# A stick-breaking attention mixer on one core: mask and sums added to the logits in PSUM, exponentials taken from there

## The chip, the cores and the metric

The kernel runs on one core of one Trainium2 chip. The metric is the device time of one execution, in microseconds. Its engines are PE (TensorE, with PEld for its weight loads), DVE (VectorE), ACT (ScalarE), POOL (GpSimd) and SP (SyncE, which issues transfers here).

## The reference

Two networks of two layers each, over 256 tokens of width 1024, batch 1, float32. The change touches one mixer, in the first layer of the first network, with 16 heads of width 64:

```python
q, k, v = jnp.split(h @ w_qkv, 3, axis=-1)     # q, k normed per head
for blk in range(2):                           # 128 queries each
    z = einsum('bhqd,bhkd->bhqk', qb, kb) / 8  # keys 0 to the block's end
    causal = kpos[None, :] < qpos[:, None]
    log_stay = where(causal, log_sigmoid(-z), 0)
    log_after = cumsum(log_stay, reverse=True) - log_stay
    weights = where(causal, exp(log_sigmoid(z) + log_after), 0)
    outs.append(einsum('bhqk,bhkd->bhqd', weights, vb))
return o @ w_o
```

Around it stand gated feed-forward layers of inner width 2816; the second network has two other attentions and a mixture of 16384 experts.

## The kernel before, in words

Each engine has its own program, written out by hand; they meet only at semaphores, and each engine works its queue in order. Weights come in units of 128 x 1024 numbers through SP's queue into a ring of six (`raw`). ACT rounds each unit to a high part (L564), DVE subtracts it for the low part (L924), and a product is three matmuls per tile, high by high, low by high and high by low (`mm3`, L1518 to L1520). ACT may run four units ahead of PE. Meanwhile POOL moves expert weights through SBUF and back to HBM during the feed-forward layers (`relay`), but not during the mixer.

The mixer follows the q, k and v products. DVE squares and sums each head (`head_norm`, L1028 to L1037), PE turns q and k, and ACT copies them out with their gains (L609). Then comes `stick_breaking`, which each of PE, ACT, DVE and POOL has under this name. The scores are kept transposed: keys on the 128 partitions, and 384 columns per head, which are queries 0 to 255 for the first 128 keys and queries 128 to 255 for the last 128 keys. Heads go in pairs p = 0 to 7, so one call on ACT, DVE or POOL covers 2 x 384 = 768 numbers per partition.

For each pair: PE forms z (L1631, L1632) in three pairs of PSUM banks, in turn. ACT takes |z| (L659), exp(-|z|) (L660) and ln(1 + that) (L664), for two pairs at a time, so that the table of activation functions is changed twice for two pairs. DVE forms max(z, 0) + ln (L1061) and min(z, 0) - ln (L1063, `logw`). POOL multiplies the first by the causal mask (L485, `stay`). PE sums it over later keys with a triangular matrix and one of ones (L1646, L1647) in banks 0 and 1, and DVE takes the sums from `logw` (L1053). When all pairs are through, a second pass starts: ACT takes Exp (L669), POOL multiplies by the mask again (L490), PE mixes the values (L1658, L1659), ACT and DVE write the high and low parts of the output (L675, L1042). After the eighth the output product starts (L1518), whose first units were split long before.

A float32 matmul (scores, sums, mixes) appears in the trace as two records with a weight load each; a matmul of high and low parts as one. The second head of a pair has q and k on partitions 64 to 127, and its mixed output goes to partitions 64 to 127.

Of the kernel before, what the change touches and what calls it, by code (L numbers as in the profile page):

```python
# [31 lines left out]
P = 128  # L32
D = 1024
T = 256
# [20 lines left out]
STICK_GROUP = 2  # L55
# [18 lines left out]
A_STICKC = 27136  # L74
# [126 lines left out]
def program(nc, stream, x_in_dram, consts, stickc, poolc, scalec, ropec, lnc, subkeys, out):  # L201
    with ExitStack() as ctx:
# [24 lines left out]
        def sem(name):  # L227
            return ctx.enter_context(nc.semaphore(name))
# [40 lines left out]
        soft_done = sem("soft_done")  # L269
        z_used = sem("z_used")  # L270
        stay_ready = sem("stay_ready")
        c_done = sem("c_done")
        c_used = sem("c_used")
        w_exp = sem("w_exp")
        w_ready = sem("w_ready")
# [43 lines left out]
        def area(at, n):  # L319
            return arena[:, at:at + n]  # L320
# [22 lines left out]
        N_PAIRS = HEADS // 2  # L343
        near = pad[:, 0:HOT * 4 * NK].rearrange("p (s n) -> p s n", n=NK)
# [40 lines left out]
        def _(pool):  # L385
# [94 lines left out]
            def stick_breaking():  # L480
                m = area(A_STICKC, PAIR).unsqueeze(1).broadcast_to([P, 2, PAIR])
                soft = blk(A_SOFT, 4, PAIR)
                for p in range(N_PAIRS):
                    pool.wait_ge(soft_done, t.after(soft_done))
                    pool.tensor_tensor(stay[:, 2 * p:2 * p + 2, :], soft[:, 2 * (p % 2):2 * (p % 2) + 2, :], m,  # L485
                                       ALU.mult).then_inc(stay_ready, 1)
                for p in range(N_PAIRS):
                    pool.wait_ge(w_exp, t.after(w_exp))
                    w = logw[:, 2 * p:2 * p + 2, :]
                    pool.tensor_tensor(w, w, m, ALU.mult).then_inc(w_ready, 1)  # L490

            for i in range(DEPTH):
# [10 lines left out]
                if i == 0:  # L503
                    power(32, 64, 32)
                    power(32, 64, 32)
                    pool.wait_ge(stick_in, t.after(stick_in, 16))
                    stick_breaking()
# [39 lines left out]
        def _(act):  # L547
# [103 lines left out]
            def stick_breaking():  # L651

                ln = blk(A_LN, 8, PAIR)
                for first in range(0, N_PAIRS, STICK_GROUP):
                    group = range(first, first + STICK_GROUP)
                    for p in group:
                        act.wait_ge(z_done, t.after(z_done))
                        m = ln[:, 2 * (p % 4):2 * (p % 4) + 2, :]
                        step(act.activation(m, ps[:, 2 + 2 * (p % 3):4 + 2 * (p % 3), 0:PAIR], ACT.Abs))  # L659
                        ins = act.activation(m, m, ACT.Exp, scale=-1.0)  # L660
                    step(ins)
                    for p in group:
                        m = ln[:, 2 * (p % 4):2 * (p % 4) + 2, :]
                        act.activation(m, m, ACT.Ln, bias=cst[:, ONE:ONE + 1]).then_inc(ln_done, 1)  # L664
                for p in range(N_PAIRS + 1):
                    if p < N_PAIRS:
                        act.wait_ge(c_used, t.after(c_used))
                        w = logw[:, 2 * p:2 * p + 2, :]
                        act.activation(w, w, ACT.Exp).then_inc(w_exp, 1)  # L669
                    if p >= 1:  # L670
                        heads_high(p - 1, 4 + (p - 1) % 4)
# [237 lines left out]
        def _(dve):  # L909
# [134 lines left out]

            def stick_breaking():
                ln, soft = blk(A_LN, 8, PAIR), blk(A_SOFT, 4, PAIR)

                def log_weights(p):

                    dve.wait_ge(z_used, t.after(z_used))  # L1050
                    dve.wait_ge(c_done, t.after(c_done))
                    w = logw[:, 2 * p:2 * p + 2, :]
                    dve.tensor_tensor(w, w, ps[:, 0:2, 0:PAIR], ALU.subtract).then_inc(c_used, 1)  # L1053

                for p in range(N_PAIRS):
                    s, r = slice(2 * (p % 2), 2 * (p % 2) + 2), slice(2 * (p % 4), 2 * (p % 4) + 2)
                    z = ps[:, 2 + 2 * (p % 3):4 + 2 * (p % 3), 0:PAIR]
                    dve.wait_ge(ln_done, t.after(ln_done))
                    if p >= 2:
                        dve.wait_ge(stay_ready, t.after(stay_ready))  # L1060
                    dve.scalar_tensor_tensor(soft[:, s, :], z, 0.0, ln[:, r, :], ALU.max,  # L1061
                                             ALU.add).then_inc(soft_done, 1)
                    dve.scalar_tensor_tensor(logw[:, 2 * p:2 * p + 2, :], z, 0.0, ln[:, r, :], ALU.min,  # L1063
                                             ALU.subtract).then_inc(z_used, 1)
                    if p >= 1:
                        log_weights(p - 1)
                t.skip(stay_ready, 2)
                log_weights(N_PAIRS - 1)
                for p in range(N_PAIRS):
                    heads_low(p, 4 + p % 4)  # L1070
# [74 lines left out]
            for i in range(DEPTH):  # L1145
# [360 lines left out]
        def _(pe):  # L1506
# [113 lines left out]
            def stick_breaking():  # L1620
                mask_tri = area(A_STICKC + PAIR, P)
                ones = area(A_STICKC + PAIR + P, P)
                pe.wait_ge(turned_kept, t.after(turned_kept, 8))
                pe.wait_ge(stick_in, 16)

                def scores(p):
                    if p >= 3:
                        pe.wait_ge(z_used, t.after(z_used))
                    for h in range(2):
                        z, r = ps[:, 2 + 2 * (p % 3) + h, :], slice(64 * h, 64 * h + 64)  # L1630
                        pe.matmul(z[:, 0:T], kT[r, p, 0:P], qT[r, p, 0:T], start=True, stop=True)  # L1631
                        ins = pe.matmul(z[:, T:PAIR], kT[r, p, P:T], qT[r, p, P:T], start=True, stop=True)  # L1632
                    ins.then_inc(z_done, 1)

                for p in range(3):
                    scores(p)
                for p in range(N_PAIRS):
                    if p + 3 < N_PAIRS:
                        scores(p + 3)

                    pe.wait_ge(stay_ready, t.after(stay_ready))
                    if p >= 1:
                        pe.wait_ge(c_used, t.after(c_used))
                    for h in range(2):
                        c, s = ps[:, h, :], stay[:, 2 * p + h, :]
                        pe.matmul(c[:, 0:PAIR], mask_tri, s, start=True, stop=False)  # L1646
                        ins = pe.matmul(c[:, P:T], ones, s[:, T:PAIR], start=False, stop=True)  # L1647
                    ins.then_inc(c_done, 1)
                t.skip(c_used)
                pe.wait_ge(z_used, t.after(z_used, 3))  # L1650
                for p in range(N_PAIRS):
                    pe.wait_ge(w_ready, t.after(w_ready))
# [459 lines left out]
```

## Time and profile before

| | us |
|---|---|
| median of 3 timed runs | 2883.92 (2879.01 to 2887.53) |
| profiled execution | 2879.02 |
| its span | 2877.1 |
| PE busy in the span | 2573.6 (89%) |
| DVE busy | 2004.7 (70%) |
| ACT busy | 1261.3 (44%) |
| POOL busy | 1170.8 (41%) |
| mean granted clock of PE | 0.963 |

The span runs from the first to the last instruction of the profiled execution; the profiled execution's own time holds what lies around it. The busy time of PE comes from matmul records that overlap, with ends that are modelled, so it says where PE is at work and not how near it is to its peak. A granted clock of 1.00 is 2.4 GHz, 0.50 is 1.2 GHz.

### The profile page before, as it was taken

The numbers are of one execution on the slowest core, as the hardware profiler recorded it, in microseconds if no ns is written. First come the engines' busy times: TensorE is split into PE (matmuls) and PEld (weight loads), VectorE is DVE, ScalarE is ACT, GpSimd is POOL, SyncE is SP. The second block draws the span as 40 slices with busy tenths as digits, with TensorE's granted clock in tenths as the row PEclk, the third lists the DMA queues.
The fourth block names the chain that finished last, engine by engine and source line by source line (L and its number), as shares of the span: only waits on it lengthen the run. The fifth ranks groups of instructions, "written<-read, shape, count | busy, mean of one in ns | idle before, by whom it ended". The sixth has DMA issues, their size and how long they took to land.

```text
span 2877.1 us, 41657 instructions
## 1 busy us (share of the span) xinstructions
PE 2573.6 (89%) x14180; PEld 2073.2 (72%) x14180; DVE 2004.7 (70%) x3942; ACT 1261.3 (44%) x2087; POOL 1170.8 (41%) x1498
## 2 busy tenths in 40 slices
PE   8999799989989987899999889999986778887776
PEld 8987589879979976699999878888774333333322
DVE  6775466756767665498899657676676767777675
ACT  5445644444444445455555445554553222222221
POOL 3531444424415431048788733332102444444442
PEclk9999899999999998799999999999898999999999
DMA  9985189989959997255555599999746999999997
GB/s 356 366 299 170 43 321 365 333 326 368 352 198 351 378 336 266 91 162 184 183 183 183 165 361 387 392 393 339 270 138 262 422 420 409 421 407 419 418 418 307
DMA packets 217960, 874.90 MB, mean 304 GB/s; under 512 B 38320, under 2 KB 38448, under 8 KB 184176
## 3 DMA queue, kind: packets, MB, share of 16 engines
q0 software_dynamic: 118640, 512.52, 46.0%
q1 hardware_dynamic: 99200, 360.96, 35.3%
q8 instruction: 54, 0.88, 0.1%
q14 instruction: 66, 0.54, 0.1%
HBM read 788.27 MB, written 152.17 MB: 327 GB/s over the span
## 4 chain that ended last, share of the span: by engine, by line
PE 56%; DMA 14%; POOL 12%; DVE 9%; ACT 4%; issue 4%; SPq 0%; POOLq 0%; DVEq 0%; ACTq 0%
PE ps L1518 16%; PE ps L1519 16%; PE ps L1520 16%; DMA arena<-both_rows,arena 12%; POOL gate_cells L447 11%; PE ps L1892 5%; DVE arena L1428 2%; DVE w_lo L924 1%; DMA raw<-in_stream 1%; PE ps L1673 1%; ACT arena L728 1%; ACT w_hi L564 1%; DVE pad L1364 0%; POOL small L391 0%; DVE act_lo L952 0%
## 5 line engine op out<-in xcount | busy, mean ns | idle before, releaser
L924 DVE TENSOR_TENSOR w_lo<-raw,w_hi 128x1024 fp32r<-128x1024 f32 x681 | 829.8, 1223 | 441.3 <-ACT w_hi L564 436.7
L564 ACT ACTIVATE w_hi<-raw 128x1024 fp32r<-128x1024 f32 x681 | 719.1, 1057 | 617.1 <-DMA raw<-in_stream 420.4
L1518 PE MATMUL ps<-act_hi,w_hi 128*128 128x256 f32 x2728 | 781.3, 286 | 7.7 <-DVE act_lo L958 3.6
L1519 PE MATMUL ps<-act_lo,w_hi 128*128 128x256 f32 x2728 | 773.7, 284 | 0.0
L1520 PE MATMUL ps<-act_hi,w_lo 128*128 128x256 f32 x2728 | 773.7, 284 | 0.0
L1892 PE MATMUL ps<-arena 128*128 128x512 f32 x1024 | 480.9, 616 | 149.0 <-ACT arena L728 148.2
L1518 PEld LDWEIGHTS ps<-act_hi,w_hi 128*128 128x128 f32 x2728 | 525.1, 192 | 18.8 <-issue 12.6
L1519 PEld LDWEIGHTS ps<-act_lo,w_hi 128*128 128x128 f32 x2728 | 525.3, 193 | 5.8 <-issue 2.6
L1520 PEld LDWEIGHTS ps<-act_hi,w_lo 128*128 128x128 f32 x2728 | 525.0, 192 | 0.0
L1892 PEld LDWEIGHTS ps<-arena 128*128 128x128 f32 x1024 | 189.2, 194 | 428.9 <-ACT arena L728 234.7
L419 POOL DMA_DIRECT2D both_rows<-arena x512 | 279.2, 552 | 411.1 <-DVE arena L990 401.2
L477 POOL DMA_INDIRECT arena<-both_rows,arena x256 | 288.4, 1126 | 385.6 <-PE ps L1892 351.0
L1428 DVE SCALAR_TENSOR_TENSOR arena<-arena 128x1024 f32<-128x1024 f32 x256 | 313.1, 1225 | 167.6 <-DMA arena<-both_rows,arena 165.9
L1518 PE MATMUL ps<-w_hi,act_hi 128*128 128x512 f32 (+1 forms) x990 | 388.3, 392 | 30.2 <-DVE act_lo L1487 16.3
L1519 PE MATMUL ps<-w_lo,act_hi 128*128 128x512 f32 (+1 forms) x990 | 385.7, 390 | 0.0
L1520 PE MATMUL ps<-w_hi,act_lo 128*128 128x512 f32 (+1 forms) x990 | 385.1, 389 | 0.0
L447 POOL DMA_INDIRECT gate_cells<-hot x256 | 317.4, 1240 | 121.4 <-issue 80.8
L1518 PEld LDWEIGHTS ps<-w_hi,act_hi 128*128 128x128 f32 x990 | 190.2, 192 | 73.5 <-issue 17.3
L721 ACT ACTIVATE hot<-hot 128x2 f32<-128x2 f32 (+1 forms) x130 | 26.4, 203 | 468.0 <-DVE arena L1428 467.3
L1520 PEld LDWEIGHTS ps<-w_hi,act_lo 128*128 128x128 f32 x990 | 189.6, 192 | 38.4
L1519 PEld LDWEIGHTS ps<-w_lo,act_hi 128*128 128x128 f32 x990 | 190.0, 192 | 37.3
L465 POOL DMA_DIRECT2D both_rows<-in_stream x128 | 68.1, 532 | 295.6 <-DMA both_rows<-in_stream 295.6
(237 smaller groups left out, 2793.5 us busy)
## 6 DMA issues: line engine op xcount, KB each, us to landing
raw<-in_stream SPq DMA_DIRECT2D x684, 512.0 KB, 5.8
arena<-in_stream POOLq DMA_DIRECT2D x128, 512.0 KB, 8.9
both_rows<-arena POOLq DMA_DIRECT2D x512, 128.0 KB, 5.9
both_rows<-in_stream POOLq DMA_DIRECT2D x128, 512.0 KB, 6.7
gate_cells<-hot POOLq DMA_DIRECT2D x32, 512.0 KB, 13.0
hot<-gate_cells POOLq DMA_DIRECT2D x128, 128.0 KB, 6.7
pad<-in_ln POOLq DMA_DIRECT2D x4, 1024.0 KB, 7.4
gate_cells<-hot POOLq DMA_INDIRECT x256
```

Source lines behind the costliest of these rows:

```text
L419: pool.dma_start(rows.rearrange("(c r) k -> r c k", r=32), arena[32 * a:32 * a + 32, A_RELAY_OUT + UNIT * s:A_RELAY_OUT + UNIT * s + UNIT] ...
L447: pool.indirect_dma_start(gate_cells[:, :], bass.IndirectOffsetOnAxis(ap=cell[:, q:q + 1], axis=0), weights[:, q:q + 1], None).then_inc(sc ...
L465: pool.dma_start(both_rows[P * n:P * n + P, D:2 * D], stream[UP_1 + n]).then_inc(up_copied[n % 2], 16)
L477: pool.indirect_dma_start(row[:, p % ROW_RING, :], None, both_rows[:, :], at).then_inc(row_in[p % ROW_RING], 16)
L564: act.activation(w_hi[:, u % SPLIT, :], raw[:, u % RAW, :], ACT.Copy).then_inc(hi_done, 1)
L728: act.activation(diags[:, p % DIAG_RING, :], ident, ACT.Copy, scale=weights[:, p:p + 1]).then_inc(diag_ready, 1)
L924: dve.tensor_tensor(w_lo[:, u % RAW, :], raw[:, u % RAW, :], w_hi[:, u % SPLIT, :].bitcast(F32), ALU.subtract).then_inc(lo_done, 1)
L1428: dve.scalar_tensor_tensor(row[:, p % ROW_RING, 0:D], row[:, p % ROW_RING, 0:D], 1.0, x_rows[:, b, :], ALU.mult, ALU.mult, accum_out=dots[ ...
L1518: pe.matmul(dst, lhs[0], rhs[0], start=first, stop=False, **kw)
L1519: pe.matmul(dst, lhs[0], rhs[1], start=False, stop=False, **kw)
L1520: return pe.matmul(dst, lhs[1], rhs[0], start=False, stop=last, **kw)
L1892: ins = pe.matmul(ps[:, 2 * (n % 2) + half, :], diags[:, p % DIAG_RING, :], row[:, p % ROW_RING, D + 512 * half:D + 512 * half + 512], sta ...
```

## The change

The logits stay in PSUM until their last use. There are four pairs of banks; pair p has pair p mod 4 of them, 384 columns of each bank for the logits and the last 128 for the output. PE adds to the logits a third matmul per head, a unit matrix times a matrix that is -2^99 where the key is not before the query. DVE writes the size of the masked logit to SBUF by clearing its sign bit (two shifts as integers); ACT takes Exp and Ln of it in place; DVE forms max(z, 0) + ln straight into `stay`, which is 0 where the mask is. PE then adds minus the sums onto the logits themselves, with a triangular matrix that includes the key's own term, so that z minus its own softplus is formed there too. ACT takes Exp from PSUM, which is the weights, and 0 where the mask is. PE mixes the values into the free columns of the same banks, in three matmuls per head, not two. Abs, the second expression on DVE, the subtraction of the sums and both multiplications on POOL are gone.

ACT goes over four pairs with each function: Exp four times, Ln four times, Exp four times with the copies between. PE forms the logits of pairs 0 to 3, then alternates sums and mixes; the logits of pairs 4 to 7 wait for the outputs of pairs 0 to 3 to have left the banks. Four small operations on DVE (`stick_terms`), before the head norms, build the matrices.

The diff is cut: removed lines that stand in the listing above are left out.

```diff
-A_STICKC = 27136
+A_STICKC, A_TERMS = 27136, 27776
...
+        stick_ring = blk(A_LN, 8, PAIR)
+        neg_tri, neg_ones = area(A_TERMS, P), area(A_TERMS + P, P)
+        neg_mask, unit_mat = in_place("neg_mask", [P, P], base + 4 * (A_TERMS + 2 * P)), in_place("unit_mat", [P, P], base + 4 * (A_TERMS + 3 * P))
+        def logit(p):
+            r = 2 * (p % 4)
+            return ps[:, r:r + 2, 0:PAIR]
+        def mixed(p):
+            r = 2 * (p % 4)
+            return ps[:, r:r + 2, PAIR:PAIR + P]
+        def sizes(p):
+            return stick_ring[:, 2 * (p % 4):2 * (p % 4) + 2, :]
...
-            def stick_breaking():
...
-                    pool.tensor_tensor(stay[:, 2 * p:2 * p + 2, :], soft[:, 2 * (p % 2):2 * (p % 2) + 2, :], m,
...
-                    pool.tensor_tensor(w, w, m, ALU.mult).then_inc(w_ready, 1)
...
-                    stick_breaking()
...
+                def weights_of(p):
+                    act.wait_ge(c_done, p + 1)
+                    act.activation(logw[:, 2 * p:2 * p + 2, :], logit(p), ACT.Exp).then_inc(w_exp, 1)
+                def output_high(p):
+                    act.wait_ge(o_done, t.after(o_done))
+                    act.activation(act_hi[:, p, :].rearrange("p (b q) -> p b q", b=TB), mixed(p),
+                                   ACT.Copy).then_inc(o_hi, 1)
+                for first in (0, 4):
+                    group = range(first, first + 4)
                     for p in group:
...
+                        act.wait_ge(size_done, p + 1)
+                        ins = act.activation(sizes(p), sizes(p), ACT.Exp, scale=-1.0)
                     step(ins)
                     for p in group:
...
+                        act.activation(sizes(p), sizes(p), ACT.Ln, bias=cst[:, ONE:ONE + 1]).then_inc(ln_done, 1)
+                    for p in group:
+                        weights_of(p)
+                        if p > first:
+                            output_high(p - 1)
+                    output_high(first + 3)
...
+            def stick_terms():
+                dve.wait_ge(stick_in, 16)
+                ahead = area(A_STICKC, P)
+                dve.tensor_scalar(neg_tri, ahead, -1.0, None, ALU.add)
+                dve.tensor_scalar(neg_mask[:, :], ahead, -1.0, 2.0 ** 99, ALU.add, ALU.mult)
+                dve.tensor_scalar(neg_ones, area(A_STICKC + PAIR + P, P), -1.0, None, ALU.mult)
+                dve.tensor_copy(unit_mat[:, :], ident).then_inc(terms_ready, 1)
             def stick_breaking():
...
+                def size(p):
+                    dve.wait_ge(z_done, p + 1)
+                    dve.tensor_scalar(sizes(p).bitcast(U32), logit(p).bitcast(U32), 1, 1, ALU.logical_shift_left,
+                                      ALU.logical_shift_right).then_inc(size_done, 1)
+                def stays(p):
+                    dve.wait_ge(ln_done, p + 1)
+                    dve.scalar_tensor_tensor(stay[:, 2 * p:2 * p + 2, :], logit(p), 0.0, sizes(p), ALU.max,
+                                             ALU.add).then_inc(stay_ready, 1)
+                def output_low(p):
+                    dve.wait_ge(o_hi, t.after(o_hi))
+                    dve.tensor_tensor(act_lo[:, p, :].rearrange("p (b q) -> p b q", b=TB), mixed(p),
+                                      act_hi[:, p, :].bitcast(F32).rearrange("p (b q) -> p b q", b=TB),
+                                      ALU.subtract).then_inc(act_ready, 1)
+                for p in range(4):
+                    size(p)
+                for p in range(4):
+                    stays(p)
+                for p in range(3):
+                    output_low(p)
+                size(4)
+                output_low(3)
+                for p in range(5, 8):
+                    size(p)
+                for p in range(4, 8):
+                    stays(p)
+                for p in range(4, 8):
+                    output_low(p)
...
+                    stick_terms()
...
             def stick_breaking():
...
                 pe.wait_ge(turned_kept, t.after(turned_kept, 8))
...
+                pe.wait_ge(terms_ready, 1)
+                def logits(p):
                     if p >= 4:
                         pe.wait_ge(act_ready, t.after(act_ready))
                     for h in range(2):
...
+                        z, r = logit(p)[:, h, :], slice(64 * h, 64 * h + 64)
+                        same = z.rearrange("p (c q) -> p c q", q=P)[:, 0:3:2, :]
+                        pe.matmul(z[:, 0:T], kT[r, p, 0:P], qT[r, p, 0:T], start=True, stop=False, skip_group_check=True)
+                        pe.matmul(z[:, T:PAIR], kT[r, p, P:T], qT[r, p, P:T], start=False, stop=False,
+                                  skip_group_check=True)
+                        ins = pe.matmul(same, unit_mat[:, :], neg_mask[:, :].unsqueeze(1).broadcast_to([P, 2, P]),
+                                        start=False, stop=False, skip_group_check=True)
+                    ins.then_inc(z_done, 1)
+                def sums(p):
+                    pe.wait_ge(stay_ready, p + 1)
+                    for h in range(2):
+                        z, s = logit(p)[:, h, :], stay[:, 2 * p + h, :]
+                        pe.matmul(z, neg_tri, s, start=False, stop=False, skip_group_check=True)
+                        ins = pe.matmul(z[:, P:T], neg_ones, s[:, T:PAIR], start=False, stop=True, skip_group_check=True)
+                    ins.then_inc(c_done, 1)
+                def mix(p):
+                    pe.wait_ge(w_exp, p + 1)
+                    for h in range(2):
+                        e, v = logw[:, 2 * p + h, :], slice(HD * (2 * p + h), HD * (2 * p + h) + HD)
+                        o = mixed(p)[64 * h:64 * h + 64]
+                        pe.matmul(o[:, 0, :], v_tok[:, 0, v], e[:, 0:P], start=True, stop=True, skip_group_check=True)
+                        pe.matmul(o[:, 1, :], v_tok[:, 0, v], e[:, P:T], start=True, stop=False, skip_group_check=True)
+                        ins = pe.matmul(o[:, 1, :], v_tok[:, 1, v], e[:, T:PAIR], start=False, stop=True,
+                                        skip_group_check=True)
                     ins.then_inc(o_done, 1)
+                for p in range(4):
+                    logits(p)
+                sums(0)
+                sums(1)
+                mix(0)
+                sums(2)
+                mix(1)
+                sums(3)
+                mix(2)
+                logits(4)
+                mix(3)
+                for p in (5, 6, 7):
+                    logits(p)
+                sums(4)
+                sums(5)
+                mix(4)
+                sums(6)
+                mix(5)
+                sums(7)
+                mix(6)
+                mix(7)
```

## Rows read from the trace of the kernel before

**Rows 1.** The page's chain that ended last, shares of the span by engine.

```profile
PE 56%; DMA 14%; POOL 12%; DVE 9%; ACT 4%; issue 4%; SPq 0%; POOLq 0%; DVEq 0%; ACTq 0%
```

**Rows 2.** Chain of waits, end of the mixer: start us, us, what.

```profile
334.13 1.81 POOL arena L490
338.50 0.79 PE ps L1518
```

**Rows 3.** Groups by line and shape, 283.5 to 338.5: line, engine, form | busy us, mean ns | idle.

```profile
L485 POOL TENSOR_TENSOR arena<-arena 128x768 f32<-128x768 f32 x8 | 14.5, 1815 | 35.4 <-DVE arena L1061 35.4
L1061 DVE SCALAR_TENSOR_TENSOR arena<-ps,arena 128x768 f32<-128x768 f32 x8 | 7.6, 953 | 15.2 <-ACT arena L664 15.2
L664 ACT ACTIVATE arena<-arena,cst 128x768 f32<-128x768 f32 x8 | 7.0, 926 | 0.0
L660 ACT ACTIVATE arena<-arena 128x768 f32<-128x768 f32 x8 | 6.7, 843 | 0.2
L659 ACT ACTIVATE arena<-ps 128x768 f32<-128x768 f32 x8 | 6.4, 798 | 1.0 <-PE ps L1632 1.0
L660 ACT ACT_TABLE_LOAD x4 | 5.1, 1283 | 0.1
L1042 DVE TENSOR_TENSOR act_lo<-ps,act_hi 128x256 fp32r<-128x256 f32 x8 | 3.4, 425 | 11.9 <-ACT act_hi L675 11.9
L675 ACT ACTIVATE act_hi<-ps 128x256 fp32r<-128x256 f32 x8 | 3.1, 383 | 13.0 <-PE ps L1659 13.0
```

**Rows 4.** Busy time by stretch: us, then PE, PEld, DVE, ACT, POOL; PE's granted clock; DMA.

```profile
284.30:293.20 8.90, 2.88 (x20) 2.59 (x16) 1.83 (x3) 8.54 (x10) 0.72 (x1) 0.51 0.00 1
293.20:298.05 4.85, 4.80 (x15) 3.21 (x16) 1.72 (x2) 4.78 (x6) 2.86 (x2) 0.50 0.00 2
298.05:322.00 23.95, 17.68 (x92) 11.98 (x90) 17.07 (x19) 19.40 (x21) 13.48 (x8) 1.00 0.00 0
322.00:332.20 10.20, 4.84 (x45) 2.87 (x46) 3.08 (x6) 5.47 (x10) 8.20 (x6) 1.00 0.01 2
332.20:338.50 6.30, 3.81 (x23) 1.84 (x19) 1.27 (x3) 1.88 (x4) 3.52 (x2) 0.50 0.00 0
338.50:342.40 3.90, 3.90 (x9) 3.13 (x10) 0.00 (x0) 0.00 (x0) 0.00 (x0) 0.50 0.00 0
```

**Rows 5.** PE's instructions in order of time, same records merged: start us, us, form, count.

```profile
283.56 0.71 PE L1631 MATMUL ps<-arena 64*128 64x256 f32 x4 [2.66 <-ACT arena L609]
298.35 0.71 PE L1631 MATMUL ps<-arena 64*128 64x256 f32 x4
298.88 0.39 PE L1632 MATMUL ps<-arena 64*128 64x128 f32 x4
299.62 0.88 PE L1646 MATMUL ps<-arena 128*128 128x384 f32 x2 [0.35 <-DVE arena L1053]
301.53 0.71 PE L1631 MATMUL ps<-arena 64*128 64x256 f32 x4
322.00 0.66 PE L1658 MATMUL ps<-arena 128*64 128x256 f32 x4
322.48 0.40 PE L1659 MATMUL ps<-arena 128*64 128x128 f32 x4
```

**Rows 6.** ACT in order of time, at the next feed-forward layer's first Silu.

```profile
371.60 1.28 ACT L639 ACT_TABLE_LOAD   x1
376.60 0.38 ACT L639 ACTIVATE arena<-ps 128x256 f32<-128x256 f32 x1 [3.72 <-PE ps L1520]
```

**Rows 7.** PE in order of time, inside a product with 256 columns.

```profile
149.75 0.28 PE L1519 MATMUL ps<-act_lo,w_hi 128*128 128x256 f32 x1
149.87 0.28 PE L1520 MATMUL ps<-act_hi,w_lo 128*128 128x256 f32 x1
```

**Rows 8.** POOL and DVE in order of time, ahead of the mixer.

```profile
205.35 0.60 POOL L499 DMA_DIRECT2D arena<-in_stick  x1 [0.15 <-issue]
235.40 2.29 DVE L1028 TENSOR_TENSOR arena<-arena 128x2048 f32<-128x2048 f32 x1 [0.60 <-ACT arena L619]
```

More of the change, by code:

```diff
@@ L268, in program @@
         ln_done = sem("ln_done")
-        soft_done = sem("soft_done")
-        z_used = sem("z_used")
+        terms_ready = sem("terms_ready")
+        size_done = sem("size_done")
         stay_ready = sem("stay_ready")
         c_done = sem("c_done")
-        c_used = sem("c_used")
         w_exp = sem("w_exp")
-        w_ready = sem("w_ready")
         o_done = sem("o_done")
@@ L478, in gather @@
                                                 at).then_inc(row_in[p % ROW_RING], 16)
-            def stick_breaking():
[L481 to L484, printed above, removed]
-                    pool.tensor_tensor(stay[:, 2 * p:2 * p + 2, :], soft[:, 2 * (p % 2):2 * (p % 2) + 2, :], m,
[L486 to L489, printed above, removed]
-                    pool.tensor_tensor(w, w, m, ALU.mult).then_inc(w_ready, 1)
             for i in range(DEPTH):
@@ L651, in stick_breaking @@
             def stick_breaking():
-                ln = blk(A_LN, 8, PAIR)
-                for first in range(0, N_PAIRS, STICK_GROUP):
-                    group = range(first, first + STICK_GROUP)
+                def weights_of(p):
[7 more added lines that the diff above has]
+                    group = range(first, first + 4)
                     for p in group:
[L657 to L660, printed above, removed]
+                        act.wait_ge(size_done, p + 1)
+                        ins = act.activation(sizes(p), sizes(p), ACT.Exp, scale=-1.0)
                     step(ins)
                     for p in group:
[L663 to L671, printed above, removed]
+                        act.activation(sizes(p), sizes(p), ACT.Ln, bias=cst[:, ONE:ONE + 1]).then_inc(ln_done, 1)
[4 more added lines that the diff above has]
+                    output_high(first + 3)
             def heads_high(k, bank):
@@ L1043, in heads_low @@
                                   ALU.subtract).then_inc(act_ready, 1)
-            def stick_breaking():
[L1046 to L1070, printed above, removed]
@@ L1620, in stick_breaking @@
             def stick_breaking():
-                mask_tri = area(A_STICKC + PAIR, P)
-                ones = area(A_STICKC + PAIR + P, P)
                 pe.wait_ge(turned_kept, t.after(turned_kept, 8))
[L1624 to L1652, printed above, removed]
+                pe.wait_ge(terms_ready, 1)
+                def logits(p):
                     if p >= 4:
@@ L1655, in stick_breaking @@
                     for h in range(2):
-                        o, e = ps[64 * h:64 * h + 64, 4 + p % 4, :], logw[:, 2 * p + h, :]
-                        v = slice(HD * (2 * p + h), HD * (2 * p + h) + HD)
-                        pe.matmul(o[:, 0:T], v_tok[:, 0, v], e[:, 0:T], start=True, stop=False)
-                        ins = pe.matmul(o[:, P:T], v_tok[:, 1, v], e[:, T:PAIR], start=False, stop=True)
-                    ins.then_inc(o_done, 1)
+                        z, r = logit(p)[:, h, :], slice(64 * h, 64 * h + 64)
```

2 lines of the change are left out of this document (removed).

## The prediction

> **What bounds the kernel now.** The page comes first. Its chain of waits [rows 1] gives PE 56% of the span; the rest is transfers and POOL in the later layers. The change touches one stage of one layer, so everything is decided between its first matmul (L1631, at 283.56 us in the instructions in order of time [rows 5]) and the first matmul of the product after it (L1518, at 338.50 in the chain of waits of that stretch [rows 2]): 54.94 us, 1.9% of the span. Grouped by line [rows 3], that stretch holds 8 calls of each form, one per head pair. ACT works 8 x (0.80 + 0.84 + 0.93) plus eight table loads of 1.28 (four at L660, as many at L664; one more at L669 later) between the first score and the last Ln, and is idle for 1.0 us: it bounds the first 31 us. Then POOL bounds: the second multiplication by the mask (L490, 1.81 each) is on the chain to 335.94 [rows 2]. PE is not the bound anywhere here. The granted clock [rows 4] fell to half (1.2 GHz) at 284.3, just after a pause of 2.66 us [rows 5]; it stayed there through 8.9 us in which PE worked 2.9, and rose at 298.05, when PE had worked without a stop since 293.2 (4.85 us). It fell again at 332.2, after 10.2 us with PE at work for 4.8, and rose at 342.4, 3.9 us into the product. DMA moves nothing in the stretch, and nothing behind it waits for an absolute time: what the stage gains, the kernel gains.
>
> **The change, part by part.**
>
> *POOL.* All 16 multiplications leave (8 x 1.82 [rows 3], and 8 of L490's 1.81 [rows 2]). The first eight lay beside ACT's work; the second eight were the bound of the last 16 us. Nothing else is moved past POOL's queue.
>
> *ACT.* Abs leaves (8 x 0.80). Exp of the size, Ln, Exp of the weights and the copies stay: 8 x (0.84 + 0.93 + 0.80 + 0.38) = 23.6. For the Exp that now reads PSUM I take L659's 0.80, which reads the same shape from there. Table loads: nine now (4 + 4 + 1), five after: Exp, Ln, Exp, Ln, Exp. A load does not wait for what its activation waits for: at L639 it ran at 371.60 and the activation came at 376.60, once PE was done [rows 6]. So the first Exp load hides behind the first logits, and those ahead of the weights behind PE's sums. Two loads, both before Ln, stay on the path. The Trainium skill (ScalarE: Activation LUTs, What ACT_TABLE_LOAD costs) gives a switch 2.66 us, as a load of 1283 ns and a drain of about 1380. The rows give 1283 ns and no drain: the activations and loads of groups of two pairs fill ACT's time. With the drain the change would save about 1.4 us more for each of seven loads that leave the path, some 10 us; this is a rival below. The same page (Table sets) says that one set holds both exp and ln; this program reloads at each turn, so the rule earns nothing here.
>
> *DVE.* L1063 and L1053 leave, the sign-clearing of 768 numbers from PSUM comes, L1061 stays. The trace has no integer shift of that size; the nearest rows are L1061 (768 from PSUM, 0.95) and L1042 (256, 0.43), so it lies between 0.8 and twice 0.95; I take 0.95. It matters only once per half. DVE has 8 x (0.95 + 0.95 + 0.43) = 18.6 us, and is no bound. The four small operations of `stick_terms` (128 columns each) cost at most 4 x 0.43, L1042's price for 256. They wait for a table that was issued at 205.4, 30 us earlier, and stand in the 0.60 us in which DVE idles ahead of L1028 at 235.40 [rows 8]. What overflows, up to 1.1 us, delays a square and the lows of the k weights, which run ahead of PE. I count nothing; without that cover it is 1.1 us.
>
> *PE.* A new load. Sums: from L1646 at 299.62 to L1631 at 301.53 a pair takes 1.91 [rows 5]; unchanged. Mixes: 0.88 a pair, from 322.00 to 322.88, the last record's tail of about 0.15 in it; the same columns in 12 passes rather than 8, so 0.75 to 1.2; I take 0.85. Logits: now the two heads of a pair lie in different halves of the array, and both run at once: four records of each kind fit into 298.35 to 299.27 [rows 5], about 0.75 without the tail. The change puts a full-height matmul (the mask, 256 columns) behind each head. One such matmul with its weights takes 0.12 (149.75 to 149.87 [rows 7]), so two take 0.24. If the heads no longer overlap, 384 columns at the sums' rate (1.91 us for 2 x 512 columns, so 0.70 for 384) make 2 x 0.70 + 0.24 = 1.64 a pair; if they still do, 1.0. Upwards, each of four changes of tile shape may cost the 0.1 that stands at the head of a run, so 2.04. I take 1.64. The Trainium skill (PSUM — Partial Sum Buffer, Engine vs sequencer instructions) says that matmuls start and complete in program order. By that the mask stands between the heads and 1.64 holds. The records speak half against it: the source issues head 0 wholly before head 1, yet the four L1631 come before the four L1632, so something ahead of the array had put them in turn. By this the price would be 1.0.
>
> *The clock.* Low stretches: the fall at 284.3 comes from what PE did before the change's first matmul, and stays. Each long PE pause makes another. I take each to last 4.4 us of steady work (between 3.9 and 4.85 [rows 4]), which costs 2.2.
>
> *The path*, since PE, ACT and DVE now take turns:
> a. Four pairs of logits: 4 x 1.64 + 2.2 = 8.8, to 292.3. ACT and DVE follow pair by pair beneath.
> b. Size of pair 3 (0.95), its Exp (0.84), the Ln load (1.28), the first Ln (0.93), the first `stays` (0.95), hand-overs 0.3: 5.25, to 297.6. PE stands still throughout.
> c. Four sums, four mixes, logits 4: 4 x 1.91 + 4 x 0.85 + 1.64 + 2.2 = 14.9, to 312.5. Each Exp of weights (0.80) fits under the next sums.
> d. Logits 5, 6, 7: 4.9, to 317.4. Each has its bank: the low halves of pairs 1 to 3 end before.
> e. As b: 5.25, to 322.7.
> f. Four sums, four mixes: 11.0 + 2.2 = 13.2, to 335.9.
> g. Last copy 0.38, last difference 0.43, hand-overs 0.3: to 337.0.
> The stage takes 53.4 instead of 54.9: -1.5. The product then starts with PE warm: its first 3.9 us at half clock [rows 4] gave up 1.95. Together -3.5 us. The profiled execution (2879.02, span 2877.1 and 1.9 around it) would become 2875.5. It equals the fastest of the three timed runs and lies 4.9 below their median; on the median the forecast is 2883.9 - 3.5 = 2880.4. So most of what ACT and POOL gave up goes to PE, with twice a chain of 5.25 us in which nothing overlaps.
>
> **The rivals.**
> 1. *The heads still run side by side.* 8 x 0.64 = 5.1 less on the path: 8.6 gained, 2875.3; with a shorter low stretch up to 11. For it: the order of the records [rows 5]. Against: a full-height matmul needs both halves in between.
> 2. *PE becomes the bound at half clock.* Place: logits 0 to 3. Half-height matmuls did not lift the clock in 284.3 to 293.2, though PE was at work for 2.9 us. If one head's half doesn't either, part a takes 0.7 + 2 x (6.56 - 0.7) = 12.4 instead of 8.8, and the gain is gone: 2883.9. From there each 0.1 a pair adds about 1.2; with 2.04 a pair the loss is about 5: 2889. It decides from 1.64 a pair and a low stretch over all four. Against it: PE has no pause in those 8 us.
> 3. *The change doesn't do what it says*: loads of tables not merged or not hidden, or the shift twice as long: two Exp loads and two sizes more on the path, 2 x 1.3 + 2 x 0.95 = 4.5 slower than forecast, 2884.9.
> 4. *A drain at each load leaves the path too*: 2871. The skill's figure speaks for it, the full ACT rows against.
>
> **How the numbers follow.** Forecast 0.50 (2877.5 to 2883.5), rival 1 0.20, rival 2 0.20, rival 3 0.07, rival 4 0.03. No change can be told from one under 0.3%, or 8.65 us, here. Half of rival 1 and all of rival 4 lie beyond it: faster 0.13. Slower takes a corner of rival 2 and the scatter of medians: 0.07. The rest, 0.80, is the same. The range is 2873 to 2889.
>
> **What would show it.** In the profile after: nothing of POOL in the stage; five table loads; PE idle for about 5 us twice, between the fourth logits and the first sums of each half; 1.6 us between the z of two pairs at full clock (1.0 for rival 1, over 1.9 for the high bound); the first sums at half clock; the product's first matmuls at full clock and about 53 us behind the first logits. A half clock up to 293 is rival 2. The prediction is wrong if the stage shrinks by over 7 us or grows, or if the time moves with the stage unchanged.

## The result, and the profile after

The changed kernel took 2894.91 us (median of 10 runs, 2884.32 to 2899.33) and the kernel before 2885.41 (10 runs, 2879.01 to 2890.69): a ratio of 1.0032, 95% interval 1.0016 to 1.0048. It is slower by 9.5 us, which is 0.3% and clear of the scatter, and outside the forecast's range of 2873 to 2889. The profiled execution took 2897.5, with a span of 2895.7.

Busy time by stretch in the profile after, with the columns of [rows 4]: six parts of the stage as the prediction cut it (a, b, c, d, e, f with g), the whole stage, and the product behind it up to the additions to x.

```profile
286.20:302.40 16.20, 16.20 (x40) 11.19 (x40) 2.87 (x3) 3.76 (x4) 0.00 (x0) 0.52 0.00 0
302.40:307.50 5.10, 0.01 (x1) 0.00 (x0) 1.90 (x3) 4.04 (x5) 0.00 (x0) 0.50 0.01 2
307.50:323.20 15.70, 15.63 (x90) 11.21 (x90) 4.82 (x8) 7.17 (x10) 0.00 (x0) 0.90 0.00 1
323.20:332.10 8.90, 8.90 (x31) 6.33 (x30) 2.35 (x4) 2.80 (x4) 0.00 (x0) 0.75 0.00 0
332.10:337.30 5.20, 0.07 (x1) 0.00 (x0) 1.94 (x3) 4.07 (x5) 0.00 (x0) 0.50 0.00 0
337.30:352.00 14.70, 13.77 (x80) 9.84 (x80) 4.27 (x7) 7.53 (x11) 0.00 (x0) 0.86 0.00 0
286.18:352.03 65.85, 54.60 (x240) 38.59 (x240) 18.15 (x24) 29.39 (x37) 0.00 (x0) 0.71 0.00 0
352.03:373.80 21.77, 21.77 (x96) 17.94 (x96) 8.58 (x8) 7.42 (x7) 0.00 (x0) 1.00 0.51 162
```

The stage took 65.85 us where it had taken 54.94: 10.9 more. The product took 21.77; in the trace of before it is this:

```profile
338.50:362.09 23.59, 23.59 (x96) 19.28 (x96) 8.58 (x8) 7.42 (x7) 0.00 (x0) 0.92 0.47 151
```

So 1.82 came back, at full clock from its first matmul. The sum, +9.1, is near the 9.5 between the medians. (The two profiled executions differ by 18.5; 2.6 of it lies ahead of the stage and 6.9 behind the product, in code that the change leaves alone.) POOL has nothing left in the stage. ACT, which bounded its first 31 us, is busy for 29.4 of 65.9 and PE for 54.6 (it was 34.8).

PE's instructions in order of time in the profile after, with the columns of [rows 5]: the first heads, then logits 4 and the first mix behind it.

```profile
286.18 0.70 PE L1651 MATMUL ps<-arena 64*128 64x256 f32 x2 [2.66 <-ACT arena L608]
286.71 0.57 PE L1652 MATMUL ps<-arena 64*128 64x128 f32 x2
287.22 0.58 PE L1654 MATMUL ps<-neg_mask,unit_mat 128*128 128x256 f32 x1
287.73 1.22 PE L1651 MATMUL ps<-arena 64*128 64x256 f32 x2
288.74 0.63 PE L1652 MATMUL ps<-arena 64*128 64x128 f32 x2
289.31 0.58 PE L1654 MATMUL ps<-neg_mask,unit_mat 128*128 128x256 f32 x1
289.82 1.22 PE L1651 MATMUL ps<-arena 64*128 64x256 f32 x2
...
320.99 0.70 PE L1651 MATMUL ps<-arena 64*128 64x256 f32 x2
321.53 0.38 PE L1652 MATMUL ps<-arena 64*128 64x128 f32 x2
321.84 0.38 PE L1654 MATMUL ps<-neg_mask,unit_mat 128*128 128x256 f32 x1
322.15 0.43 PE L1671 MATMUL ps<-arena 128*64 128x128 f32 x2
```

The reader is to see two things. In [rows 5] four L1631 stand in one record and four L1632 in the next: both heads of a pair ran at once. Here two stand together, then two, then a mask: one head wholly before the other. And a head takes 2.09 us at half clock (287.73 to 289.82) and 1.16 at full (320.99 to 322.15), so a pair takes 4.18 or 2.32.

### The profile page after: what moved, and what is told of

It is laid out like the page before. It is cut to its first block, busy times and chain, and to the rows that moved or that the text cites. A ratio compares the mean times of both kernels' runs of the same rounds, so it can differ in the third digit from the quotient of the medians.

```text
span 2895.7 us, 41694 instructions
## 1 busy us (share of the span) xinstructions
PE 2597.0 (90%) x14228; PEld 2092.9 (72%) x14228; DVE 1996.0 (69%) x3938; ACT 1250.7 (43%) x2075; POOL 1141.8 (39%) x1482
## 4 chain that ended last, share of the span: by engine, by line
PE 57%; DMA 14%; POOL 12%; DVE 9%; issue 4%; ACT 4%; SPq 0%; POOLq 0%; DVEq 0%; ACTq 0%
PE ps L1537 16%; PE ps L1538 16%; PE ps L1539 16%; DMA arena<-both_rows,arena 12%; POOL gate_cells L460 11%; PE ps L1929 4%; DVE arena L1447 2%; DMA raw<-in_stream 1%; PE ps L1710 1%; DVE w_lo L926 1%; ACT w_hi L563 1%; ACT arena L730 1%; PE ps L1651 1%; PE ps L1662 1%; ACT arena L598 0%
## 5 line engine op out<-in xcount | busy, mean ns | idle before, releaser
L1537 PEld LDWEIGHTS ps<-act_hi,w_hi 128*128 128x128 f32 x2728 | 527.1, 193 | 17.8 <-issue 12.5
L1537 PEld LDWEIGHTS ps<-w_hi,act_hi 128*128 128x128 f32 x990 | 189.5, 191 | 75.5 <-issue 21.3
L404 POOL TENSOR_TENSOR small<-small,cst 128x1 f32<-128x1 f32 (+2 forms) x27 | 26.9, 998 | 475.7 <-DVE small L936 394.2
```

Source lines behind the costliest of these rows:

```text
L1537: pe.matmul(dst, lhs[0], rhs[0], start=first, stop=False, **kw)
```

## The experiments

"The stage" is always the stretch from its first logits (or scores) matmul to the first matmul of the product, in the profiled execution; it was 54.94 before and 65.85 after. It is compared between all kernels, and it is one execution each, so a difference of 2 us between two stages can be chance (see "When the clock rises" below). Times are compared only with the runs of the kernel before on the same chip: on the chip of the first seven kernels these took about 2985 us, on those of the last four about 2884.

The theory: the mask between the two heads of a pair puts them one after the other, and PE, at work with one half-height head at a time, doesn't bring its clock up. The rivals: the two mask matmuls are dear in themselves; the clock was low from before and only stays so; four pairs per table make a hand-over that is too long.

**Masks behind both heads.** The same matmuls in another order:

```diff
     for h in range(2):
         ...
         pe.matmul(z[:, T:PAIR], kT[r, p, P:T], qT[r, p, P:T], start=False, ...)
-        ins = pe.matmul(same, unit_mat[:, :], ...)
+    for h in range(2):
+        same = logit(p)[:, h, :].rearrange("p (c q) -> p c q", q=P)[:, 0:3:2, :]
+        ins = pe.matmul(same, unit_mat[:, :], ...)
```

> The changed kernel with one edit: the mask matmuls of a pair come after both heads' logits, not one behind each head. The stage from the first logits to the first matmul of the product took 65.9 us in the changed kernel (54.9 in the kernel before); a pair of logits 4.18 us at half clock and 2.32 at full. Theory A (the mask between the heads keeps them from running side by side): a pair falls to about 1.25 us at full clock and 2.5 at half, four pairs from 16.2 to about 9 us, the stage to 54 to 57 us, the time to about that of the kernel before (2884 to 2888). Rival B (the price is that of the mask matmuls themselves and of changing the shape of the tile, in whatever order): a pair stays over 2.0 at full clock and the stage at 63 to 66 us, the time at 2893 to 2896.

The stage took 51.70, 14.2 less than after, and less than the 54 to 57 expected. The time was 2977.56 (median of 12 runs) against 2983.24 for before, ratio 0.9999 (0.9961 to 1.0036): the same as before, as expected. In its order of time, and in a stretch of its first logits:

```profile
287.78 0.71 PE L1650 MATMUL ps<-arena 64*128 64x256 f32 x4
288.31 0.40 PE L1651 MATMUL ps<-arena 64*128 64x128 f32 x4
288.64 0.50 PE L1655 MATMUL ps<-neg_mask,unit_mat 128*128 128x256 f32 x2
289.07 0.71 PE L1650 MATMUL ps<-arena 64*128 64x256 f32 x4
...
283.67:290.40 6.73, 6.73 (x40) 5.02 (x40) 2.87 (x3) 3.17 (x4) 0.00 (x0) 0.75 0.00 0
```

Four and four records again, 1.29 a pair at full clock instead of 2.32, the four pairs in 6.73 us instead of 16.2 (9 were expected); and the clock rose 3.7 us after the first of them. The masks themselves take 0.43 of the 1.29. The whole loss goes with the order of two instructions.

**No masks.**

```diff
-    pe.matmul(z[:, T:PAIR], kT[r, p, P:T], qT[r, p, P:T], start=False, ...)
-    ins = pe.matmul(same, unit_mat[:, :], ...)
+    ins = pe.matmul(z[:, T:PAIR], kT[r, p, P:T], qT[r, p, P:T], start=False, ...)
```

> The changed kernel without the mask matmuls (the causal mask is left out of the computation). Theory A: a pair of logits takes 0.7 us at full clock and 1.3 at half, as the scores did before; stage 51 to 53 us. Rival B: the same shrinkage, since it gives all of it to the masks; the two differ in how far this run lies below the one with the masks last: about 4 to 6 us by A, over 10 by B.

The stage took 48.00 and a pair 1.28 at half clock, 0.66 to 0.75 at full; 2959.64 us in one run. The stage is 3.7 us shorter than with the masks last, so the 16 masks cost 0.46 a pair; the other 14.2 us came from where they stood. By the mask-price rival this run had to lie over 10 below the one with the masks last. The stage is shorter than the 51 to 53 expected, as that of the run with the masks last was.

**Clock up before the logits.** Eleven full-height matmuls of 512 columns in the pause ahead of the first logits, into a bank that they overwrite:

```diff
+    pe.wait_ge(turned_kept, t.after(turned_kept, 4))
+    for _ in range(11):
+        pe.matmul(ps[:, 4, :], unit_mat[:, :], neg_mask[:, :].unsqueeze(1).broadcast_to([P, 4, P]), start=True, stop=True)
```

> The changed kernel with eleven full-height matmuls of 512 columns (mask by unit matrix, overwritten afterwards) in PE's pause of 2.66 us ahead of the logits. Theory A2 (one half-height head after another does not hold the clock up): the level doesn't fall at the first logits, but falls within 3 to 8 us of logits work all the same, as it did at 327.4 us of the changed kernel; stage 60 to 64 us. Rival C (it is the pause before that costs the level; once up it stays up while PE works): four pairs at 2.32 us are 9.3 us, the level stays at full to the end of the fourth pair, the stage takes 57 to 59 us.

```profile
281.86 2.79 PE L1645 MATMUL ps<-neg_mask,unit_mat 128*128 128x512 f32 x11 [0.34 <-ACT arena L608]
284.59 0.70 PE L1655 MATMUL ps<-arena 64*128 64x256 f32 x2
...
281.00:284.50 3.50, 3.16 (x16) 2.27 (x14) 0.00 (x0) 3.48 (x7) 0.00 (x0) 1.00 0.00 0
284.50:289.00 4.50, 4.50 (x20) 3.38 (x19) 0.96 (x1) 1.76 (x2) 0.00 (x0) 0.94 0.00 0
289.00:293.20 4.20, 4.20 (x12) 2.93 (x11) 0.96 (x1) 0.84 (x1) 0.00 (x0) 0.50 0.00 0
```

The logits began at full clock and stayed there for 3.9 us. Then, at 288.5, the clock fell, with PE at work in every part of both stretches (4.50 of 4.50, 4.20 of 4.20), and stayed low for the rest of them. The stage took 62.93, only 2.9 less (3024.64 us in one run). So the low clock isn't only inherited: these heads, one after the other and with nothing else between, don't hold it. The profile after has the same once more, at 327.7, in the middle of logits 5 to 7 (323.2 to 332.2), where PE had no pause either.

**The kernel before, with the masks.** Its scores get a mask matmul behind each head and nothing else is changed:

```diff
-    ins = pe.matmul(z[:, T:PAIR], kT[r, p, P:T], qT[r, p, P:T], start=True, stop=True)
+    pe.matmul(z[:, T:PAIR], kT[r, p, P:T], qT[r, p, P:T], start=False, stop=False, ...)
+    ins = pe.matmul(same, unit_mat[:, :], neg_mask[:, :].unsqueeze(1).broadcast_to([P, 2, P]), start=False, stop=True, ...)
```

> The kernel before with one part of the change alone: the mask matmul behind each head's scores (and the two small operations that build its matrices); everything else as before, the later multiplications by the mask too. Theory A: scores of a pair cost 4.2 us at half clock and 2.3 at full here too, but there ACT paces the stage at 3.8 us a pair, so only part shows: stage 55 to 60 us, with the three first pairs of scores taking 12 us and not 3. By rival B the same. If the scores keep their 0.7 to 1.3 us a pair, both are wrong and the price comes from something else in the change (the banks shared with the outputs, or the waits).

```profile
282.36 1.22 PE L1642 MATMUL ps<-arena 64*128 64x256 f32 x2
283.37 0.63 PE L1643 MATMUL ps<-arena 64*128 64x128 f32 x2
283.94 0.58 PE L1644 MATMUL ps<-neg_mask,unit_mat 128*128 128x256 f32 x1
284.44 1.22 PE L1642 MATMUL ps<-arena 64*128 64x256 f32 x2
...
280.73:302.00 21.27, 19.56 (x49) 13.41 (x49) 3.55 (x4) 13.55 (x15) 3.58 (x2) 0.52 0.00 1
301.80:316.00 14.20, 14.11 (x64) 10.14 (x63) 9.83 (x11) 12.20 (x14) 5.46 (x3) 1.00 0.00 0
```

Four scores and the first sums now keep PE busy for 19.6 of 21.3 us, at half clock, and ACT, which had filled this stretch, works 13.6 of it. The stage took 65.59 (2992.58 us in one run), well over the 55 to 60 expected: the loss of the change, made in the kernel before by two matmuls a pair. The last line shows the limit of the clock's part. From 301.8 to 316.0 the heads still go one after the other, but each pair of them is followed by full-height sums, and the clock stayed at full through 14.1 us of work. It is long stretches of such heads alone that ran at half clock.

**Two pairs in rotation.** With the masks fixed, PE still stands for 5.2 us twice. First attempt: ACT, DVE and PE go round by two pairs instead of four, with nine table loads.

```diff
     for p in range(4):
         logits(p)
+    for p in (0, 2, 4, 6):
+        sums(p)
+        sums(p + 1)
+        mix(p)
+        mix(p + 1)
+        if p < 4:
+            logits(p + 4)
+            logits(p + 5)
```

> The mask matmuls behind both heads (stage 51.7 us in the run with that edit alone), and the order of all three engines rolled by two pairs: ACT takes Exp of the sizes of pairs 2 and 3 with the weights of 0 and 1 under one table, then Ln of 2 and 3 under the other, and so on; PE sums and mixes two pairs between logits. Nine table loads again in place of five. Theory A (what is left on the path after the order of the masks is the chain size, Exp, load, Ln, stays of 5.2 us in which PE stands still, twice): the chain shrinks at its head and vanishes later; ACT then bounds, with 8.4 us per two pairs: stage 41 to 46 us, the time 9 to 13 us below the kernel before. Rival D (fewer table loads are what the change gains): four loads of 1.28 more on ACT's queue: stage 53 to 57.

> The same rolled order, with the mask matmuls behind each head as in the changed kernel. Theory A: PE needs 2.3 + 1.9 + 1.1 = 5.3 us a pair at full clock and the first four logits still take 16 us at half clock, so the stage lies between 52 and 58 us: below the changed kernel's 65.9, but 9 us or more above the run with both edits. If the order of the masks matters little once the chain is shortened (rival), it lies within 3 us of that run.

Both missed: with the masks last (f1) 50.30, ratio 0.9962 (0.9924 to 1.0001), and with the masks between (f2) 66.55, 2998.24 us in one run. The rotation cut PE's long pauses into several short ones, and in f1 the clock was low four times; its mean over the stage was 0.83, so low for some 17 us in all. In f2 PE is busy for 59.5 of the 66.6 us: while the heads go one after the other, PE is the bound, and this order of the tables doesn't help.

**Two pairs per table.** The masks last and all else as after, but ACT turns from Exp to Ln after pairs 0 and 1:

```diff
-    for p in group: ... ACT.Exp ...
-    for p in group: ... ACT.Ln ...
+    for two in (group[0:2], group[2:4]):
+        for p in two: ... ACT.Exp ...
+        for p in two: ... ACT.Ln ...
```

> The masks behind both heads, and one part of the change undone: ACT changes its table every two pairs (Exp, Exp, Ln, Ln, twice per half), nine loads in place of five; DVE and PE as they were. Rival D (table loads are on the path): two loads more per half, 2.6 us each time: stage 55 to 57 us against 51.7. Theory A (the first Ln is what PE waits for, and it now comes after two Exp and not four): the first sums start 2.6 us earlier in each half, the weights about 2 us: stage 47 to 50 us.

49.91, as expected: 1.8 less than with four pairs per table, with four table loads more, where the load rival had 3 to 5 more. The first sums came 10.2 us behind the first logits instead of 11.9, although the first logits took 1.5 us longer here, their clock rising later. What counts is when the first Ln comes, for which PE waits. (2990.48 us in one run; the stage is what is compared.)

**Clock held through the pauses.** Two pairs per table, the eleven matmuls ahead of the logits (g0), and then also six float32 matmuls of 128 columns ahead of the first sums of each half (g1):

```diff
+    for _ in range(6):
+        pe.matmul(mixed(p)[:, 0, :], neg_tri, v_tok[:, 0, 0:P], start=False, stop=False, ...)
     sums(0)
```

> The masks behind both heads and two pairs per table (stage 49.9 us), with work that only keeps PE busy: eleven full-height matmuls of 512 columns in the pause ahead of the logits, and six of 128 columns in float32 into unused columns of a bank (overwritten later) in the pause ahead of the first sums of each half. Theory A2 (a pause, or half-height work alone, brings the clock down, and the low stretches cost the stage about 3.5 us in the first logits, 2 and 3 us in the sums after the pauses): level at full through the logits and nearly all sums, stage 42 to 46 us, and the time 9 to 13 us below the kernel before. Rival (the low stretches lie beside ACT's and DVE's work and cost nothing by now): stage 48.5 to 51.

> The same with only the eleven matmuls ahead of the logits. Theory A2: four pairs of logits, side by side by twos, hold the level (they fill both halves of the array): 1.29 us a pair, 5.2 us for four; the first sums start about 2 us earlier than without, stage 46 to 48.5 us. If half-height work is too little even side by side, the level falls during the logits as it did with the masks between, and the stage stays at 49 to 50.

g0: stage 48.71, 1.2 less than without and just over the range (2876.46 us in one run). Its four pairs of logits stayed at full clock, but the clock was low again in the first sums. g1 missed: 53.80. Against before it came to 2879.44 over 2885.70, ratio 0.9977 (0.9961 to 0.9992). Its order of time on PE and ACT:

```profile
293.96 0.81 PE L1671 MATMUL ps<-arena 128*128 128x384 f32 x2
294.61 0.38 PE L1672 MATMUL ps<-arena 128*128 128x128 f32 x2
...
295.24 1.76 ACT L670 ACTIVATE arena<-arena,cst 128x768 f32<-128x768 f32 x2
297.02 1.28 ACT L655 ACT_TABLE_LOAD   x1
298.31 1.51 ACT L655 ACTIVATE arena<-ps 128x768 f32<-128x768 f32 x2
...
301.13 1.65 PE L1671 MATMUL ps<-arena 128*128 128x384 f32 x2
```

The sums ran early and at full clock, and PE then stood until ACT had done Ln of pairs 2 and 3, loaded a table and taken the first weights. In that new pause the clock fell, and the next two records of the sums took 1.65 where two had taken 0.81. Holding the clock in one pause had moved the pause.

**Rotation and clock together.** The f1 order, both outputs ahead of the next two Ln, so that ACT keeps going (h2); the same with the eleven and six extra matmuls, ahead of the logits and of sums 0 (h1):

```diff
     output_high(p - 2)
+    output_high(p - 1)
     size_ln(p)
-    output_high(p - 1)
     size_ln(p + 1)
```

> The masks behind both heads, the order rolled by two pairs (stage 50.3 us, of which four stretches at half clock), with two edits: both outputs of a group leave before the next two Ln, so that both next logits can start together; and the work that keeps PE busy, eleven matmuls ahead of the logits and six in the first pause. Theory A2 (half clock after each pause is what holds the rolled order at 50 us; ACT's 8.4 us per two pairs are the floor): at most one low stretch, stage 41 to 45 us, the time 10 to 14 us below the kernel before. Rival E (the chain of hand-overs from ACT to PE to DVE and back inside each group of two pairs, 11.5 us in that run, holds it up, whatever the clock): stage 47 to 50 us.

> The same order without the work that keeps PE busy. A2: half clock returns in the first logits, the first sums and later; stage 47 to 51 us, 4 us or more above the other run of this call. E: within 2 us of it.

h1 took 2871.44 against 2881.96 for before: ratio 0.9952 (0.9932 to 0.9971), the fastest version of those measured over several runs. Its stage is 45.16, at the upper end of what A2 gave; without the extra matmuls (h2) it is 49.75, within its range, and the time of one run 2872.54. That is no more than the scatter away from h1, so only the stage tells the two apart. Stretches of h1 (its stage up to the fall of the clock, and the low stretch), and the stage of h2:

```profile
283.77:321.80 38.03, 30.26 (x218) 22.84 (x218) 17.12 (x22) 31.39 (x37) 0.00 (x0) 1.00 0.00 1
321.80:325.00 3.20, 3.20 (x9) 2.20 (x8) 0.00 (x0) 0.81 (x1) 0.00 (x0) 0.50 0.00 0
```

```profile
285.93:335.68 49.75, 40.18 (x241) 29.17 (x241) 17.87 (x24) 34.30 (x41) 0.00 (x0) 0.83 0.00 0
```

With the extra matmuls the clock is low for about 3.4 us of the stage; without them its mean is 0.83, so low for some 17 us. The stages differ by 4.6 us, and 3.7 of that lies in the first four pairs of logits (5.2 us in h1, 8.98 in h2). ACT is busy for 31.4 of the first 38.0 us: the stage is near ACT's own work again, as it was before, but now without the multiplications on POOL and the eight Abs.

**When the clock rises.** Five kernels with the two heads of a pair side by side enter the logits behind the same pause of about 2.7 us, without extra matmuls. With the masks last the clock came back 3.7 us after the first logits, and without masks after 4.0. With f1 and with two pairs per table it took 7.8 us, and in h2 the level did not come back within the four pairs at all. The four pairs of f1, and those of h2, from first start to last end:

```profile
285.21:293.46 8.25, 8.25 (x40) 6.07 (x40) 2.87 (x3) 5.43 (x6) 0.00 (x0) 0.59 0.00 1
285.93:294.91 8.98, 8.98 (x40) 6.56 (x40) 2.87 (x3) 5.65 (x6) 0.00 (x0) 0.52 0.00 1
```

The matmuls are the same as those that took 6.76 us with the masks last. So heads side by side are no promise of a quick rise, and up to 2.2 us between any two of these stages is only when it came in the first logits. What stands is the contrast: heads one after the other, alone on PE, never brought the level up in 16 us (after, and f2 at a mean of 0.51 over 16.57 us), and it fell from full in the middle of their work. The order of the masks is worth more than the scatter: 14.2 us here, and 66.55 against 50.30 in f2 and f1. What about these heads brings the clock down is not shown. They use half of the array, and they also leave time unused between short matmuls (a head takes 1.16 us at full clock, where 0.82 was worked out); no run separates the two.

## Why the prediction was wrong, by its own steps

- *PE, logits: "I take 1.64"* is the first term that failed: 2.32 at full clock. The mechanism was the one that was taken (the mask stands between the heads, so they no longer overlap, by the order of the records above); its size was beyond even the upper bound of 2.04. At full clock a head is 0.54 for z[:, 0:T], 0.31 for z[:, T:PAIR] and 0.31 for the mask. By the terms of the forecast they were 0.47, 0.23 and 0.12: there are 0.07, 0.08 and 0.19 more, at each of the three, not only where the tile shape changes. Over the eight pairs this is 8 x 0.68 = 5.4 us. The row taken for the mask [rows 7] is the pace inside a run of full-height matmuls; even two masks in a row cost 0.43 behind the heads (288.64 to 289.07 with the masks last), for 0.24.
- *The clock: "4.4 us of steady work"* is the second, and the larger: 6.6 us in a and d. It stayed low for all of term a, and fell again in term d while PE worked. Rival 2 had this for a ("12.4 instead of 8.8"), argued from the half-height matmuls of [rows 4], and was given 0.20 because PE has no pause there. That was the wrong reason to discount it: a busy PE isn't enough. The two together: a 16.2 instead of 8.8, of which 4 x 0.68 = 2.7 is the price at full clock and 4.7 the level; d 8.9 instead of 4.9, of which 2.0 and 1.9.
- *Terms b and e*: 5.2 and 5.2 for 5.25. PE stood for 5.16 us each time:

```profile
307.57 1.65 PE L1662 MATMUL ps<-arena 128*128 128x384 f32 x2 [5.16 <-DVE arena L1066]
```

- *Term c*: 15.65 for 14.9: logits 4 at 2.32 makes 0.7 of it; mixes at 1.07 a pair (322.15 to 323.22), not 0.85, make 0.9 (within the stated 0.75 to 1.2); against it 0.8 less for the sums, whose low stretch was 3.1 us and not 4.4. *f and g*: 14.7 for 14.3, the mixes. All other terms together are off by 1.1; the logits in a and d by 11.4, and 11.4 + 1.1 = 12.5 is what lies between the 53.4 forecast and 65.85. The time moved by 9.5 where -3.5 was forecast; the stage explains 12.5 of these 13.0.
- *ACT*: five loads, the Exp load hidden. From the groups of the stage by line and form, and ACT's order of time:

```profile
L668 ACT ACT_TABLE_LOAD x2 | 2.6, 1283 | 0.0
L654 ACT ACT_TABLE_LOAD x2 | 2.6, 1283 | 0.0
L665 ACT ACT_TABLE_LOAD x1 | 1.3, 1283 | 0.0
...
286.14 1.28 ACT L665 ACT_TABLE_LOAD   x1
290.92 0.84 ACT L665 ACTIVATE arena<-arena 128x768 f32<-128x768 f32 x1 [3.49 <-DVE arena L1061]
```

The load ran 4.8 us ahead of its activation, as [rows 6] had it. Rival 4 is out: no drain shows; the Ln load starts at 304.29, behind an activation that ended at 304.27, and its own activation at 305.59. The Trainium skill (ScalarE: Activation LUTs, What ACT_TABLE_LOAD costs) adds about 1380 ns per switch; these rows show 1283 ns and nothing beside it.
- *DVE*: the sign-clearing took 0.957, for 0.95. Its group in the stage, with those of the sums (whose idle time of 10.3 is the two pauses) and of the masks (510 ns a record, the mean over both clocks, against 0.28 us in [rows 7]):

```profile
L1662 PE MATMUL ps<-arena 128*128 128x384 f32 x32 | 16.6, 605 | 10.3 <-DVE arena L1066 10.3
L1654 PE MATMUL ps<-neg_mask,unit_mat 128*128 128x256 f32 x16 | 8.2, 510 | 0.0
L1061 DVE TENSOR_SCALAR arena<-ps 128x768 uint32<-128x768 uint32 x8 | 7.7, 957 | 26.2 <-PE ps L1654 26.2
```

- *`stick_terms` at nothing*: right. Its four operations lie in DVE's idle time ahead of L1030, which starts 1.83 us after the start of the low-part difference ahead of it (236.18), as its like did in the kernel before (233.57 to 235.40):

```profile
237.32 0.22 DVE L1052 TENSOR_SCALAR arena<-arena 128x128 f32<-128x128 f32 x1
237.73 0.22 DVE L1055 CAST unit_mat<-cst 128x128 fp32r<-128x128 f32 x1
238.01 2.29 DVE L1030 TENSOR_TENSOR arena<-arena 128x2048 f32<-128x2048 f32 x1
```

- *The product starts warm*: yes, worth 1.82 for 1.95.
- Rival 1 (side by side, for which "something ahead of the array had put them in turn") fell. What that something is, stays open: no run here shows why two heads of different halves are interleaved and why the mask ends it. The masks-last order shows that two full-height matmuls behind four half-height ones leave the four interleaved. By the Trainium skill (PSUM — Partial Sum Buffer, Engine vs sequencer instructions) matmuls start and complete in program order; the trace agrees as far as the mask, which no record of the next head passes, and not for the two heads ahead of it, whose records are interleaved.

The chances failed where the range did: the argument had the right place and the right sign for the loss (rival 2, up to 2889) and then let "PE has no pause" take the weight from it. By its own line of 8.65 us, the 9.5 measured is "slower", which had 0.07.

## What to carry to other kernels

Treat matmuls that share the array by halves as one unit: here the two full-height masks behind both heads cost 0.46 us a pair, and one of them between the heads sent the stage from 51.7 to 65.9. Before giving a stretch to PE at full clock, ask what kind of work fills it, not only whether it is busy. And where three engines take turns, fewer table loads in larger groups can lengthen the one hand-over that PE waits for; a clock gained in one pause can be lost in the next, as in g1.

## What the hardware showed that was not expected

- Half-height float32 heads one after another, a mask between them, left the granted clock at half through all but the start of 16.2 us of unbroken work (286.2 to 302.4, mean 0.52), and let it fall from full under unbroken work (at 327.7 after, at 288.5 with the extra matmuls ahead). With full-height sums between the pairs, such heads ran at full clock for 14.1 us. Two heads at a time, the clock rose after 3.7 to 7.8 us in four kernels and not within 8.98 us in a fifth, and the three kernels that entered the logits with a high clock and paired heads (g0, g1, h1) kept it through them.
- A head and its mask took 1.16 us at full clock where 0.82 was worked out from columns and pace; with heads paired, 1.29 us held two heads and two masks.
